# GpSimd's expert-row gathers issued from loops on the engine, with their indices copied into a ring of four lists

## What is computed

```
def peer_ffn(x, w_q, sub_keys, u, v):
    ...
    experts = jnp.take_along_axis(cand_i..., best_pos, axis=-1)   # 128 per token
    gate = jax.nn.softmax(best_s, axis=-1)
    ...
    h = jax.nn.gelu(jnp.einsum('ted,td->te', u[ec], xc))
    return jnp.einsum('te,ted->td', gc.astype(h.dtype) * h, v[ec])
```

## Time and profile before

| | |
|---|---|
| median of 3 runs | 2522.19 us (2518.62 to 2525.67) |
| the profiled execution | 2530.18 us, its span 2528.1 us |
| TensorE busy | 2149.1 us (85%), mean granted clock 0.931 |
| VectorE busy | 1415.3 us (56%) |
| ScalarE busy | 880.9 us (35%) |
| GpSimd busy | 1155.1 us (46%), 1131.2 us of it in 1024 gathers |
| DMA | 754.69 MB, of it 544.05 MB on GpSimd's queue |

### The profile page before, as it was taken

How to read it: one execution, slowest core, us unless ns; L and a number is a source line. 1 busy time by engine, 2 the same in 40 slices (tenths; PEclk the granted TensorE clock), 3 DMA queues, 4 the chain that set the end, 5 groups by cost and what they waited for, 6 DMA issues and landing times.

```text
span 2528.1 us, 24194 instructions
## 1 busy us (share of the span) xinstructions
PE 2149.1 (85%) x7260; PEld 1254.8 (50%) x7260; DVE 1415.3 (56%) x2996; ACT 880.9 (35%) x2125; POOL 1155.1 (46%) x1076
## 2 busy tenths in 40 slices
PE   7889999799999876798977998887798898667776
PEld 5667878678876542453433444343345343222232
DVE  3474554554565468674575644486635466674433
ACT  3445444644534321462222252233234223222121
POOL 0100000000000047687667667767667767777765
PEclk9999999899999799899999999998899899988898
DMA  8315545055445389899999999999999999999997
GB/s 302 146 67 183 191 174 186 31 175 195 170 146 204 113 327 353 287 338 405 415 409 371 409 410 344 413 413 398 371 414 342 377 412 368 361 323 369 378 354 299
DMA packets 172681, 754.69 MB, mean 299 GB/s; under 512 B 19184, under 2 KB 19344, under 8 KB 152736
## 3 DMA queue, kind: packets, MB, share of 16 engines
q0 software_dynamic: 148640, 544.05, 56.3%
q1 hardware_dynamic: 21584, 197.14, 21.0%
q10 hardware_dynamic: 2352, 12.24, 1.3%
HBM read 752.28 MB, written 4.22 MB: 299 GB/s over the span
## 4 chain that ended last, share of the span: by engine, by line
PE 51%; POOL 12%; DVE 11%; issue 10%; DMA 9%; ACT 3%; another core or an unknown queue 3%; DVEq 1%; ACTq 0%; POOLq 0%; SPq 0%
PE ps L906 15%; POOL Z L2262 12%; PE ps L651 7%; PE ps L652 7%; PE ps L653 7%; PE ps L926 7%; DMA Z<-v,experts 5%; DVE Z L1917 4%; DMA Z<-u,experts 3%; DMA ring<-panels 1%; PE ps L1046 1%; DVE ring_lo L1748 1%; PE ps L641 1%; PE ps L981 1%
## 5 line engine op out<-in xcount | busy, mean ns | idle before, releaser
L906 PE MATMUL ps<-Z 128*128 128x512 f32 x2048 | 995.7, 642 | 259.7 <-DMA Z<-v,experts 175.8
L906 PEld LDWEIGHTS ps<-Z 128*128 128x128 f32 x2048 | 410.0, 206 | 808.1 <-issue 566.3
L1917 DVE CUSTOM_DVE_ANT_0 Z<-Z,xn 128x1024 f32<-128x1024 f32 x512 | 609.6, 1225 | 311.8 <-DMA Z<-u,experts 256.7
L2262 POOL DMA_INDIRECT Z<-u,experts x512 | 561.9, 1097 | 329.1 <-issue 157.3
L2262 POOL DMA_INDIRECT Z<-v,experts x512 | 569.3, 1112 | 262.8 <-issue 126.0
L1748 DVE TENSOR_TENSOR ring_lo<-ring,ring_hi 128x1024 fp32r<-128x1024 f32 x212 | 247.6, 1221 | 195.1 <-ACT ring_hi L1212 194.8
L926 PE MATMUL ps<-ring,o 128*128 128x512 f32 x560 | 251.9, 602 | 2.7 <-issue 1.9
L651 PE MATMUL ps<-ring_hi,xT_lo 128*128 128x512 f32 x592 | 237.4, 401 | 13.7 <-DVE xT_lo L1796 7.3
L652 PE MATMUL ps<-ring_lo,xT 128*128 128x512 f32 x592 | 233.0, 394 | 0.0
L653 PE MATMUL ps<-ring_hi,xT 128*128 128x512 f32 x592 | 232.8, 393 | 0.0
L1212 ACT CAST ring_hi<-ring 128x1024 fp32r<-128x1024 f32 x212 | 208.9, 1051 | 37.8 <-DMA ring<-panels 35.2
(11 more groups left out here) (262 smaller groups left out, 2025.6 us busy)
## 6 DMA issues: line engine op xcount, KB each, us to landing
ring<-panels SPq DMA_DIRECT2D x106, 1024.0 KB, 5.0
ring<-panels SPq DMA_DIRECT2D x40, 2048.0 KB
Z<-u,experts POOLq DMA_INDIRECT x512
Z<-v,experts POOLq DMA_INDIRECT x512
gain<-gains ACTq DMA_DIRECT2D x4, 1024.0 KB, 4.5
pj<-keys ACTq DMA_DIRECT2D x4, 1024.0 KB
bias_lines<-bias_line POOLq DMA_DIRECT2D x1, 3072.0 KB, 17.2
gain<-gains ACTq DMA_DIRECT2D x5, 512.0 KB, 3.6
```

What stands on the lines that cost most here:

```text
L906: last = mm(ps[:, c, :], diag[s], vrow[s][:, c * NC:(c + 1) * NC], start=slot == 0, stop=slot == SLOTS - 1)
L1917: v.tensor_tensor_reduce(out=urow[s], in0=urow[s], in1=xn[:, t, :], scale=1.0, scalar=0.0, op0=ALU.mult, op1=ALU.add, accum_out=hdot[:, t, ...
L2262: g.indirect_dma_start(out=rows[s], out_offset=None, in_=tables[layer], in_offset=bass.IndirectOffsetOnAxis(ap=experts[:, t, slot:slot + 1 ...
```

## The change

GpSimd no longer has 1024 gathers written out one by one. The first four ticks of u rows and three of v rows are written out (`first_rows`), then a loop of 15 passes handles four ticks a pass (32 gathers) for layer 0, four ticks at the change of tables are written out, a second loop of 15 passes does layer 1, and the last v tick ends it. An instruction in a loop needs a fixed address for its indices. So VectorE copies the four columns of a tick from `experts` to one of four places of `listed`, `list_rows(tick)`: for ticks 0 and 1 ahead of the first dots, from then on two ticks ahead, behind `expert_dots(tick)` and ahead of the side work. It waits until the v gathers of the tick that had the place before have landed. GpSimd waits for that copy (`rows_listed`) in place of `routed`; waits in the loops are on register values, each with `apart`. The order of the gathers and both rings stay.

```diff
+LISTS, LISTED_AHEAD = 4, 2
...
+        listed = sb("listed", [P, LISTS, SLICE], U32)
...
+        rows_listed = sem("rows_listed")
...
+            def list_rows(tick):
+
+                t, at = tick // TICKS % TILES, tick % TICKS * SLICE
+                if tick >= LISTS:
+                    for n in range((tick - LISTS) * SLICE, (tick - LISTS + 1) * SLICE):
+                        dve.wait_ge(v_landed[n % RING], 16 * (n // RING + 1))
+                v.tensor_copy(listed[:, tick % LISTS], experts[:, t, at:at + SLICE]).then_inc(rows_listed, 1)
...
             steps.upto(-1)
+            for tick in range(LISTED_AHEAD):
+                list_rows(tick)
             for tick in range(len(WINDOWS) * TICKS):
                 expert_dots(tick)
+                if tick + LISTED_AHEAD < len(WINDOWS) * TICKS:
+                    list_rows(tick + LISTED_AHEAD)
                 steps.upto(tick)
...
-            def gather(rows, tables, there, tick):
-
-                layer, t = WINDOWS[tick // TICKS]
+            def u_rows(layer, tick, place):
+
+                apart(pool, (rows_listed, tick + 1))
+                for b in range(SLICE):
+                    s = (place * SLICE + b) % RING
+                    apart(pool, (u_used, tick * SLICE + (b + 1 - RING)))
+                    g.indirect_dma_start(out=urow[s], out_offset=None, in_=(u0, u1)[layer],
+                                         in_offset=bass.IndirectOffsetOnAxis(ap=listed[:, place, b:b + 1], axis=0))\
+                        .then_inc(u_landed[s], 16)
+
+            def v_rows(layer, tick, place):
...
+            def first_rows(rows, table, there, tick):
+
                 for n in range(tick * SLICE, (tick + 1) * SLICE):
-                    s, slot = n % RING, n % SLOTS
                     if n >= RING:
                         pool.wait_ge(u_used if rows is urow else v_used, n - RING + 1)
...
-            for tick in range(-1, len(WINDOWS) * TICKS):
-
-                after = tick + 1
-                if after < len(WINDOWS) * TICKS:
-                    pool.wait_ge(routed, piece_of(after // TICKS, after % TICKS * SLICE))
-                    gather(urow, (u0, u1), u_landed, after)
-                if tick >= 0:
-                    gather(vrow, (v0, v1), v_landed, tick)
+            for tick in range(LISTS):
+                pool.wait_ge(rows_listed, tick + 1)
+                first_rows(urow, u0, u_landed, tick)
+                if tick > 0:
+                    first_rows(vrow, v0, v_landed, tick - 1)
+            turn = TILES * TICKS // LISTS
+            with pool.Fori(1, turn) as i:
+                for k in range(LISTS):
+                    u_rows(0, i * LISTS + k, k)
+                    v_rows(0, i * LISTS + (k - 1), (k - 1) % LISTS)
+            for k in range(LISTS):
+                u_rows(1, turn * LISTS + k, k)
+                v_rows(k > 0, turn * LISTS + k - 1, (k - 1) % LISTS)
+            with pool.Fori(turn + 1, 2 * turn) as i:
+                for k in range(LISTS):
+                    u_rows(1, i * LISTS + k, k)
+                    v_rows(1, i * LISTS + (k - 1), (k - 1) % LISTS)
+            v_rows(1, 2 * turn * LISTS - 1, LISTS - 1)
```

More of the change, by code:

```diff
@@ L2253, in stage_pairs @@
                         last.then_inc(staged, 1)
-            def gather(rows, tables, there, tick):
-                layer, t = WINDOWS[tick // TICKS]
+            def u_rows(layer, tick, place):
[7 more added lines that the diff above has]
+            def v_rows(layer, tick, place):
+                for b in range(SLICE):
+                    s = (place * SLICE + b) % RING
+                    apart(pool, (v_used, tick * SLICE + (b + 1 - RING)))
+                    g.indirect_dma_start(out=vrow[s], out_offset=None, in_=(v0, v1)[layer],
+                                         in_offset=bass.IndirectOffsetOnAxis(ap=listed[:, place, b:b + 1], axis=0))\
+                        .then_inc(v_landed[s], 16)
+            def first_rows(rows, table, there, tick):
                 for n in range(tick * SLICE, (tick + 1) * SLICE):
-                    s, slot = n % RING, n % SLOTS
                     if n >= RING:
                         pool.wait_ge(u_used if rows is urow else v_used, n - RING + 1)
-                    g.indirect_dma_start(out=rows[s], out_offset=None, in_=tables[layer],
-                                         in_offset=bass.IndirectOffsetOnAxis(ap=experts[:, t, slot:slot + 1], axis=0))\
-                        .then_inc(there[s], 16)
+                    g.indirect_dma_start(out=rows[n % RING], out_offset=None, in_=table,
+                                         in_offset=bass.IndirectOffsetOnAxis(
+                                             ap=listed[:, tick, n % SLICE:n % SLICE + 1], axis=0))\
+                        .then_inc(there[n % RING], 16)
             for (step, arg), meets in zip(SCHEDULE, MEETS):
```

## The result

The changed kernel takes 2573.81 us (median of 4, 2559.14 to 2575.26) against 2520.4 for the kernel before beside it: a ratio of 1.0198, 95% interval 1.0158 to 1.0238, or **53 us slower** where 22.5 were forecast. The time lies inside the range, the direction is right, and the size is more than twice what the sum gave. The profiled execution took 2572.76 us, its span 2570.7.

A forecast was written before the change was run, and what follows sets the result against it. In the gather phase DMA, POOL's gathers and VectorE were taken to limit in turn. Terms 6.2 + 3.7 + 12.6 = 22.5 us on 2522.2 gave 2544.7 us, 0.9% slower, range 2524 to 2582.

The forecast's parts named there:

- POOL's own instructions: Gathers' separate register waits and loop branches on POOL: cost 0, bounds 12 us faster to 18 us slower.
- I take 0: The cost forecast for POOL's separate waits and loops: 0 us, since a wait not waited for vanishes in the pitch.
- each pass begins with a stall: Rival, chance 0.08: each of 30 loop passes stalls on instruction fetch, 1.6 us each, 48 us in all, 2593 us.
- The later release: First u gather of a tick waits for all four dots and the copy: net 2.1 us, six counted, +12.6 us.
- POOL's delay shows only once, at its end: In VectorE's own stretch, 900 to 1115 us, four release waits of 2.1 us were to count as one.
- The late start: Gathers' first ticks: first gather at 922.7 us, first dot at 928.0 for 921.8, +6.2 us, nothing given back later.
- The copies: 128 more VectorE copies of 0.17 us, counting only where VectorE is the limit, 22 ticks: +3.7 us.
- Same: the phase is DMA's: Rival, chance 0.12: in the gather phase 413 GB/s is the only limit, late start made up, 2522 us.
- Collisions go away: Rival, chance 0.11: fewer gathers stretched under dots, 169 us falls, deciding from 23 us; at a quarter, 2503 us.
- The release counts everywhere: Rival, chance 0.10: all 17 release waits cost 2.1 us, plus 0.1 us per TensorE-bound v gather, 2578 us.
- the checks named: Trace signs: first dot near 928 us, 128 copies, POOL's waits 3.6 us longer; wrong if mean gather under 1.05 us.

The follow-up runs named there:

- e3: Kernel before with every gather's wait as an instruction of its own, constant values, gathers written out; quiet chip: 2450.03 us, ratio 0.9999.
- e16: Changed kernel with a ring of eight lists filled three ticks ahead and first lists copied early, against the kernel before; held chip: 2520.54 us, ratio 1.0060.
- e9: Changed kernel with a ring of eight lists filled three ticks ahead and first lists copied early, against the kernel before; quiet chip: 2451.53 us, ratio 1.0003.
- e6: Changed kernel with both loops written out, separate waits kept but against constants, beside the kernel before; held chip: 2543.69 us, ratio 1.0142.
- e7: Changed kernel with the release undone (ring of eight lists filled three ticks ahead, 64 gathers a pass), against the kernel before; held chip: 2531.16 us, ratio 1.0094.
- e5: The changed kernel itself run again, against the kernel before; held chip: 2552.6 us, ratio 1.0185.
- e10: Kernel before with its first gather held until VectorE has ranked the second head; quiet chip: 2458.66 us, ratio 1.0030.
- e4: Kernel before with the 128 VectorE copies and their waits for landed v rows, read by nobody; quiet chip: 2451.78 us, ratio 0.9999.
- e17: Kernel before with the 128 VectorE copies and their waits, nobody waiting for them; held chip: 2519.56 us, ratio 0.9977.
- e13: Kernel before with its first gather held until VectorE has ranked the second head; held chip: 2515.98 us, ratio 1.0042.
- e12: The changed kernel itself run again, against the kernel before; quiet chip: 2464.25 us, ratio 1.0060.
- e1: Kernel before with its first gather held until VectorE has finished the side work ahead of the first dots; quiet chip: 2460.11 us, ratio 1.0033.

## Why the prediction was right in direction and wrong in size

**The failed step** is *POOL's own instructions*, "I take 0". The loop of the earlier trace rows showed rightly that a wait that is not waited for vanishes: the plain gap is 0.30 us in after too. It says nothing of a wait that is waited for. In the kernel before, 47 of the 97 v gathers that waited for TensorE began exactly 0.27 us after the end of the last matmul that frees their row. In after the commonest delay is 0.81 us (23 of 59), and with separate constant waits alone it is 0.81 us too (66 of 122 in e3). One pair of each, the kernel before and e3, TensorE's row then POOL's:

```profile
1396.46 6.46 PE L906 MATMUL ps<-Z 128*128 128x512 f32 x8 [1.11 <-issue]
...
1403.19 0.94 POOL L2262 DMA_INDIRECT Z<-v,experts  x1 [1.89 <-PE ps L906]
```
```profile
1441.56 1.98 PE L906 MATMUL ps<-Z 128*128 128x512 f32 x4 [1.48 <-DMA Z<-v,experts]
...
1444.35 0.93 POOL L2262 DMA_INDIRECT Z<-v,experts  x1 [2.53 <-PE ps L906]
```

From 1402.92 to 1403.19 is 0.27 us, from 1443.54 to 1444.35 0.81. The upper end that I had put at 0.16 us a wait should have been 0.54. The term measured 15 us (9 to 21) on a held chip (e16, with the copies in it), where I had 0 in the forecast and 18 as the upper end; separate waits alone made 6.5 of it. Between the forecast of 22.5 and the 46 to 50 us of the whole on held chips this is the largest shown part. On quiet chips "I take 0" came true (e9), and the whole of 15 us lay under the forecast. What comes with the loops has no known mechanism: no wait at the end of a pass shows it. Of the 28 returns in after, 21 have a gap of 0.30 to 0.31 us, and of the others the two of 3.68 and 3.69 us stand at the same gathers in e6, without a loop, at 3.62 and 3.63. That disposes of the rival *each pass begins with a stall*. By the rule of the Trainium skill ("Runtime: NRT & Kernel Launch", Instruction fetch mechanics) the target of this short body stays in its window, and the trace agrees. One bound of this term was also added up wrongly: 283.3 us less 895 gaps of 0.30 us is 15 us, not 12.

**The later release** is the largest term, and its size was charged to too few waits. Its mechanism holds: waits for a list last 5.4 us on average (123.9 over 23) in place of 3.6, with the stretched gathers' part given back. Measured: 8 us on quiet chips, 10 added and 23 undone on held ones, against 12.6. What failed is "POOL's delay shows only once, at its end": the table by ticks has 5.3 us at tick 4 and some 22 from tick 20 on, 17 us where I charged one wait of 2.1. The other parts of the change are in these 17 us too; undoing the release (e7 against e5) takes away 10 us between ticks 4 and 5. VectorE idles there more after the change: at 1050 to 1100 us it is busy 24.16 us where the earlier trace rows has 34.09, though the stretch holds partly other ticks. So VectorE alone did not set this stretch.

**The late start** was near: 6.2 forecast, 7 to 10.5 added. The first dot came at 926.14, not 928, and 1.7 us of the difference were there before any gather; from the first `experts` write it is 6.0 us later than before. Within the term two errors nearly cancelled: the gather began 0.5 us after the end of the ranking where I had 0.9, and from it to the dot it took 6.0 us where I had 5.3. Added alone the start is not given back later: on one chip e10 is 6.4 us behind e9 (which takes as long as the kernel before) at tick 0 and 11 at tick 127. Undone on a held chip it was 17 us, with an uncertainty of 11.

**The copies** are free in both groups. What my 3.7 us missed was not shown; likely the dot behind a copy waited for its row anyway.

**The rivals.** *Same: the phase is DMA's* is wrong even on quiet chips, where DMA is nearly full: 0.6%. *Collisions go away* happened in part: 35 us fewer of the 169, more than the 23 from which I let it decide, and the kernel was still slower. POOL now spends 62 us more waiting for VectorE (123.9 for 61.5). That the freer gathers are those behind such a wait, so that a saved us buys little, is likely and was not tried. *The release counts everywhere* named 2578 us and is the nearest; it priced the release too high, and right in kind were its separate cost for gathers that wait for TensorE and its release in VectorE's stretch.

**Against the checks named.** 413 GB/s in full stretches, 128 copies of 0.17 us and the pitch of 1.25 us came as said. POOL's waits for VectorE grew from 17 to 23, each 1.8 us longer and not 3.6. First gather and dot came 2 us sooner than said, 1.7 of it from before the gathers. The mean gather fell to 1.07 us ((554.3 + 510.6 + 19.1 + 11.9) / 1024), not under 1.05.

## What to carry to other kernels

When a list or flag for a group replaces a release item by item, the first item of each group waits for the last of the one before; fill the lists one group further ahead than the ring of rows holds (here three ticks ahead for two ticks of rows), so that the old release decides. On quiet chips a ring of eight lists filled three ahead, with the first lists copied as soon as their data exists, made the same loops free (1.0003); on held chips 0.6% stayed. A separate wait is free while nothing is waited for, and a gather that did wait began 0.54 us later behind it (0.81 for 0.27): price the two kinds apart, by the count of true waits. And the same change cost 0.60% on one chip and 1.85% on another: repeat a small loss on more than one.

## What the runs showed of the hardware that was not expected

**Two groups of chips.** The first 900 us are nearly alike: the first gather stands at 896.87 us in e4, quiet, and at 896.13 in e17, the same kernel on a held chip. The gather phase is not: in the same kernel its first dot to its last take 1510 us in e10, quiet, and 1574 in e13, held. On held chips VectorE's drains inside the ranking last on with nothing left to finish. A drain (`dve.drain()` in the kernel) stands between two dependent steps; in the quiet traces its record ends with the work before it, and in the ranking the next instruction follows 0.07 us later. Worked out from the records: 25 of them are held over 0.5 us in the kernel before, 51 us in all and up to 7.3; 13 to 33 in the held traces, 19 to 59 us; not one in the eight traces from quiet chips. All lie behind the first gather. They are not the whole difference between the groups: e5 has 19 us of them and after 59, in the same kernel, and both are far above the 2464 us of e12. In the groups by line it is one row, the second MAX8 of a ranking (idle time and "issue" at the end), in the kernel before and in e1:

```profile
L1849 DVE MAX8 ranks<-ranks 128x8 f32<-128x128 f32 x64 | 15.6, 286 | 16.7 <-issue 14.7
```
```profile
L1851 DVE MAX8 ranks<-ranks 128x8 f32<-128x128 f32 x64 | 15.6, 285 | 2.3
```

14.7 us against none, for the same 64 instructions. One such hold in the kernel before, in VectorE's timeline:

```profile
2208.04 0.29 DVE L1845 FIND_INDEX8 ranks<-ranks,ksc 128x8 uint32<-128x128 f32 x1
...
2215.95 0.49 DVE L1849 MAX8 ranks<-ranks 128x8 f32<-128x128 f32 x2 [7.38 <-issue]
```

**Gathers that start late.** On held chips 20 to 31 v gathers in each trace begin over 2 us after the last matmul that frees their row, with POOL idle ahead of them (37 to 73 us in all; 25 and 57 us in the kernel before). On quiet chips there are 0 to 2. In the kernel before the row of the gather at 2367.80 was freed 15.5 us earlier, at 2352.3, while the semaphore's update is recorded at 2367.77, and the view can name no releaser on the core:

```profile
2363.54 1.21 POOL L2262 DMA_INDIRECT Z<-v,experts  x1 [1.41 <-PE ps L906]
2367.80 0.94 POOL L2262 DMA_INDIRECT Z<-v,experts  x1 [3.05 <-remote]
```

Waits of v gathers put down to "remote" (no instruction of this core ended there) are 33.8 us in the earlier trace rows and stand in none of the quiet traces. Holds of both kinds sometimes end together: POOL's at 1397.7 and 2221.8 us, VectorE's at 1397.2 and 2221.5. Whether the chip, the time, or something beside the kernel holds them was not tried, and the cause is open. TensorE's granted clock is lower in the gather phase there too (0.90 to 0.93, against 0.93 to 0.95 in the quiet traces, both 0.95 to 0.96 before it); whether that is a cause or follows from TensorE's idling was not tried either. With them DMA is full less often (0.95 to 0.97 at 2350 us in before and after, 1.03 in e12), which fits that a delay of POOL is dearer there.

**A gather under a dot** is stretched: 1.2 to 2 us for 0.94, the longer the earlier in the dot it starts. In the kernel before, 178 gathers that started under a dot and took over 1.15 us all ended 0.8 us after that dot; in e10, quiet, 142 did (the earlier trace rows show one). The Trainium skill ("GPSIMD Engine Reference", Specifications) says that GpSimd's access to SBUF is shared with VectorE, with contention where a VectorE instruction has two SBUF inputs, as the dot has; the traces agree: in the kernel before 162 gathers took over 1.3 us, 143 of them started under a dot, and the 162 make 146 of the 169 us.
